# Prompt attention tiles in the order 7, 6, 3, 4, 5, 2, 1, 0, beside a decode whose page loads fill the DMA engines

## The reference, cut to what matters

```python
def diff_attend(q, k, v, q_pos, k_pos, lam):
    s = jnp.einsum('bqhmd,bkhmd->bhmqk', q, k) * (DK_A ** -0.5)
    p = jax.nn.softmax(jnp.where(k_pos[None, :] <= q_pos[:, None], s, -jnp.inf), axis=-1)
    w = p[:, :, 0] - lam * p[:, :, 1]
    return jnp.einsum('bhqk,bkhd->bqhd', w, v)
```

## Time and profile before

| | |
|---|---|
| median of three runs | 973.56 us (973.18 to 977.53) |
| profiled execution: own time / span | 979.25 us / 977.6 us |
| mean granted TensorE clock | 0.986 |
| busy: TensorE, VectorE, ScalarE, GpSimd | 912.6, 493.8, 391.9, 108.9 us |
| moved by DMA | 142.38 MB, 146 GB/s over the span |
| units 8 to 11 (tile 5) on TensorE | 579.07 to 628.79 us |
| units 16 to 19 (tile 3) on TensorE | about 18 us, 670 to 688 us |

### The profile page before, as it was taken

The page is one execution under the profiler, slowest core; times in us unless marked ns, Lnnn a source line. Parts: engine busy times, 40 slices in busy tenths (PEclk is TensorE's granted clock), DMA queues, the critical chain, the costliest instruction groups (busy, mean ns, idle before and its releaser), DMA issues.

```text
span 977.6 us, 18760 instructions
## 1 busy us (share of the span) xinstructions
PE 912.6 (93%) x7095; PEld 738.0 (75%) x7095; DVE 493.8 (51%) x1091; ACT 391.9 (40%) x840; POOL 108.9 (11%) x233
## 2 busy tenths in 40 slices
PE   4989979999999999998789999998979999999996
PEld 3889979999988888887456667775657787587884
DVE  5634744555574355454455655556556444444223
ACT  5533353433335643433544454445554322332211
POOL 1300000000000000002000004343011000000000
PEclk9999999999999999999999999999998999999998
DMA  7362216222332222222976779986984621303221
GB/s 230 96 176 66 66 45 150 67 65 66 97 98 82 86 65 66 86 66 72 357 255 184 240 229 336 334 302 222 319 280 161 234 87 70 95 25 124 86 97 44
DMA packets 115555, 142.38 MB, mean 146 GB/s; under 512 B 9719, under 2 KB 76151, under 8 KB 115466
## 3 DMA queue, kind: packets, MB, share of 16 engines
q1 hardware_dynamic: 109706, 122.31, 39.0%
q0 software_dynamic: 5760, 18.88, 5.4%
HBM read 125.34 MB, written 15.41 MB: 144 GB/s over the span
## 4 chain that ended last, share of the span: by engine, by line
PE 82%; ACT 5%; DMA 4%; DVE 3%; SPq 3%; issue 2%; POOL 0%; POOLq 0%; ACTq 0%; DVEq 0%
PE ps L2003 71%; PE ps L2006 11%; DMA Vr<-in_cache_v 2%; DMA Kr<-in_cache_k 1%; SPq L608 1%; DMA xrow<-in_x_prompt 1%; PE ps L1998 1%; ACT U L955 1%; DMA wst<-in_w_in 0%; ACT whi L930 0%; SPq L598 0%; ACT wh L971 0%; ACT junk L1250 0%; DVE pp L1797 0%; ACT pp L1172 0%
## 5 line engine op out<-in xcount | busy, mean ns | idle before, releaser
L2003 PE MATMUL ps<-hhi,whi 128*128 128x272 f32 (+1 forms) x672 | 227.0, 338 | 2.0 <-DVE hlo L1317 2.0
L2003 PE MATMUL ps<-hhi,wlo 128*128 128x272 f32 (+1 forms) x672 | 217.5, 324 | 0.0
L2003 PE MATMUL ps<-hlo,whi 128*128 128x272 f32 (+1 forms) x672 | 217.0, 323 | 0.0
L2003 PE MATMUL ps<-wh,r 128*128 128x512 f32 x512 | 146.6, 402 | 0.7 <-DVE wout_lo L1863 0.6
L2003 PEld LDWEIGHTS ps<-hhi,whi 128*128 128x128 f32 x672 | 127.2, 189 | 14.8 <-issue 3.7
L2003 PEld LDWEIGHTS ps<-hlo,whi 128*128 128x128 f32 x672 | 127.5, 190 | 9.9 <-issue 1.9
L2003 PEld LDWEIGHTS ps<-hhi,wlo 128*128 128x128 f32 x672 | 127.0, 189 | 9.3
L2003 PEld LDWEIGHTS ps<-wh,r 128*128 128x128 f32 x512 | 95.8, 190 | 23.3 <-issue 1.9
L1333 DVE TENSOR_TENSOR wlo<-wst,whi 128x1024 fp32r<-128x1024 f32 x56 | 68.8, 1229 | 82.0 <-ACT whi L930 82.0
L1762 DVE COPY kTs<-ps 128x512 f32<-128x512 f32 x64 | 44.1, 689 | 71.2 <-PE ps L2006 71.1
L2006 PEld LDWEIGHTS ps<-ident,Kr 128*128 128x128 f32 x512 | 57.1, 143 | 29.2 <-issue 22.0
(11 more groups left out here) (371 smaller groups left out, 1356.5 us busy)
## 6 DMA issues: line engine op xcount, KB each, us to landing
Kr<-in_cache_k SPq DMA_DIRECT2D x128, 256.0 KB, 4.1
wst<-in_w_in SPq DMA_DIRECT2D x56, 512.0 KB, 3.7
Vr<-in_cache_v POOLq DMA_DIRECT2D x72, 256.0 KB, 4.6
Vr<-in_cache_v SPq DMA_DIRECT2D x56, 256.0 KB, 4.4
out_y_prompt<-rows SPq DMA_DIRECT2D x16, 512.0 KB, 2.9
xrow<-in_x_prompt SPq DMA_DIRECT2D x8, 512.0 KB, 4.8
wout<-in_w_out SPq DMA_DIRECT2D x8, 512.0 KB, 5.7
rows<-in_x_prompt SPq DMA_DIRECT2D x8, 512.0 KB, 4.4
```

Of the source, the lines that this page charges most:

```text
L2003: return nc.tensor.matmul(out, lhsT, rhs, start=start, stop=stop, **more)
```

## The change

One line: the list of query tiles. PARTS, DECODED, ATTEND, VALUES_BEFORE and OT are worked out from it.

```diff
 UNITS = CH * H
 PART = 512
-TILES = [7, 6, 5, 4, 3, 2, 1, 0]
+TILES = [7, 6, 3, 4, 5, 2, 1, 0]
 PARTS = [-(-(TILES[u // H] + 1) * P // PART) for u in range(UNITS)]
```

## The result

| | before | after |
|---|---|---|
| median of the runs taken together, us | 974.51 (21 runs, 970.63 to 980.02) | 979.15 (21 runs, 974.01 to 987.31) |
| profiled execution: own time / span, us | 979.25 / 977.6 | 977.63 / 976.0 |

The ratio is 1.0047, 95% interval 1.0029 to 1.0065: 4.6 us slower (2.8 to 6.3). That is clear of zero, and still under the 0.5% that the prediction took for measurable. The forecast was +1.2 us; the median lies inside its range of 970 to 980 us and outside its middle band of 973 to 976.5.

The account below looks back on a forecast made before the run. The prediction took TensorE, with 82% of the chain, to bound the kernel, with DMA close in the key stretch. Its terms, 0 + 0.5 + 5.6 - 2.6 - 2.3 = +1.2 us, gave 974.8 us, range 970.0 to 980.0 us.

Parts of the forecast that it names:

- Point 1: TensorE work moved from units 8 to 13 into units 16 to 21: 5.0 us each way, sum 0.
- Point 2: Key stretch, units 8 to 13: DMA engines full but buffers cover; +0.5 us (0 to +4).
- the +0.5 us for uneven loads: Key stretch: the allowance for uneven loads, with DMA engines expected to be full.
- its 61.5 us for the stretch: Key stretch: time for 22.0 MB at about 358 GB/s, 1.4 us more than TensorE needs.
- The rival of stalled keys: Key stretch: landings pass 10.2 us and TensorE stalls for keys; 978.3 us at the upper end, chance 0.14.
- Point 3: Two-part units 16 to 19 among value steps each wait 1.40 us before second scores; +5.6 us (+1.6 to +6.1).
- Point 4: Units 16 to 21: waits for `head_weights` and value pages go, `wT` waits return in 20 and 21; -2.6 us (-3.0 to -1.0).
- Point 5: Last stretch, after value step 47: SyncE's queue limits the gain to -2.3 us (-3.0 to -0.9).
- the 0.85 us of unit 23's scores: Unit 23's 384-column scores now come behind value step 47, so that step ends 0.85 us sooner.
- The clock falls in units 16 to 19: Units 16 to 19: repeated 1.4 us waits bring two clock falls of some 1.3 us; 977.4 us, chance 0.15.
- The loads run ahead: Last stretch nearly free, second-score waits 0.7 us each; 968.9 us, chance 0.14 in part, 0.07 in full.

Follow-up runs that it names:

- e10: Tile order 7, 6, 2, 1, 5, 4, 3, 0 in place of the kernel before's order, for a lighter key part; 981.84 us in one execution.
- e3: Changed kernel, with VectorE writing the first half of `pp` after only the first part's turning; 976.88 us, ratio 1.0009 to the kernel before.
- e1: Kernel before with tiles 5 and 4 exchanged, inside the key part; 976.75 us, ratio 1.0000.
- e2: Kernel before with tiles 4 and 3 exchanged, so units 16 to 19 have parts of 512 and 128 columns; 979.2 us, ratio 1.0031.
- e11: Changed kernel again with no edit, for a second profile; 983.67 us in one execution.
- e5: Changed kernel with SyncE loading page numbers for value steps 52 to 63 ahead; 978.4 us, ratio 1.0001 to the kernel before.
- e7: Changed kernel with both edits of e3 and e5; 975.06 us, ratio 0.9979 to the kernel before.
- e12: e7 again without further edit, in another session; 974.07 us, ratio 1.0003 to the kernel before.
- e4: Changed kernel with GpSimd issuing value pages up to step 47 instead of 35; 981.2 us, ratio 1.0048 to the kernel before.
- e9: Changed kernel with phase 2's value step or weight turning moved to phase 3 in units 15 to 19; 980.56 us, ratio 1.0046 to the kernel before.
- e6: Kernel before with SyncE loading page numbers ahead, the same edit as e5; 976.59 us, ratio 1.0007.

## Why the prediction came out as it did

**What bounds the kernel** held: TensorE has 84% of the chain (82% before), and each of the differences above is a wait of TensorE or its own work.

**Point 1, right.** The work that left the key part is 5.06 us (4.43 in the stretch and 0.63 ahead of it), forecast 5.0. In the two value stretches busy time grew by 5.18 us (4.64 + 0.54).

**Point 2, key stretch: near in the sum, by luck.** The key step of unit 13 was to come 4.5 us sooner after that of unit 8, and came 4.43 sooner. Two errors offset each other. No part of it was a stall: TensorE lacks 0.42 us there before and after, so the +0.5 us for uneven loads didn't come. And I took the whole 5.0 us of moved work between the borders, though 0.63 us of it lies ahead of the first. The DMA engines took the pace: 384 GB/s at a share of 1.03 over 10 us.

```profile
600.00:610.00 10.00, 10.00 (x130) 7.24 (x132) 5.64 (x14) 4.28 (x9) 3.51 (x7) 1.00 1.03 384
```

The Trainium skill, page "DMA: Bandwidth & Descriptors", section Specifications, gives about 358 GB/s from HBM for a core; the 384 GB/s lie above it, and its 61.5 us for the stretch did not come (60.62). The rival of stalled keys is refuted for this order; e10, one execution, shows it begun at 3.5 us less work.

**Point 3, right.** Four new waits of 1.40 us, 5.6 us in all; with unit 15's, 7.0. The timeline of e3 shows the cause, the waits of e1 and e2 that it belongs to a pair among value steps. One slip: by L1789 the turning that VectorE waits for in unit 15 is that of unit 13's weights, where I wrote 14; the times read are those of the right rows.

**Point 4, nearly right.** The waits for `head_weights` and pages went, as forecast, and the `wT` waits came back in units 20 and 21, but as 0.91 and 0.47 us where I had put them at the old size. That was 0.52 and 0.37 us; the one of unit 16 isn't quite alike, as I had it. Idle time in the value stretch grew by 3.3 us (7.06 less 3.80) against 3.0 forecast, busy time by 4.6 against 4.15.

**Point 5 failed, and it is most of the miss of the first profile.** TensorE's idle time in the last stretch is 5.35 us, and it was 5.36. Of the forecast -2.3 us only 0.3 came (+0.53, less the 0.85 us of unit 23's scores). The mechanism named was right: the stretch is the start of SyncE's queue on step 51, the queue's time from there, and the way from its last issue to the last value step.

| | start | queue | to the last value step |
|---|---|---|---|
| before | 0.8 | 24.3 | 3.7 |
| forecast | 0.2 | 23.5 | 3.7 |
| after | 0.2 | 25.3 | 3.9 |
| after, second profile (e11) | 0.2 | 24.8 | 4.2 |

The step that failed is "I take the lower end". The working gave 23.5 to 24.9 us for the queue, and I chose 23.5 on the argument that its waits for used buffers would go, as TensorE would free them early and run at full speed. In the first profile 2.0 us of such waits are left in the 25.3. But e11 and e3 have only 0.2 us of them, and their queues still take 24.8 and 24.4 us: even without these waits the lower end wasn't reached. What in the queue's own work takes the rest isn't shown.

Two other things differ from the forecast in the first profile. TensorE waited 1.5 us for `on`, the chain of ScalarE's squares, GpSimd's root and VectorE's scale for the prompt's rows, for which the kernel before waits only 0.3 us between 655 and 738 us; and a page wait of 1.76 us was followed by half speed from 723.4 to 726.8, as 1.80 us was before. Neither explains the length: e3 and e11 run at a clock of 1.00 through the whole stretch, wait 0.6 and 0.9 us for `on`, and take 29.0 and 29.1 us, nearly the 29.4 of the first profile. e5, e7 and e12 show the queue's part: with the numbers ahead the same stretch is 2.9, 3.3 and 2.4 us shorter, of which some 1.2 us come back among the value steps ahead of it (46.03 and 45.90 us in e7 and e12, 44.76 in e3).

**The rivals.** "The clock falls in units 16 to 19", given 0.15, is partly true. Of the four profiles of the changed order with full 1.40 us waits three have a stretch of 3.4 us at 0.50 among value steps 27 to 47 (e11 from 677.6, e4 from 682.3, e5 from 674.7) and one, the first, has none. Of the four with the waits of units 16 to 19 cut to 0.55 to 1.10 us (e3, e7, e9, e12) none has one. e10, in another order, has five full waits in a row and no fall. A fall costs 1.6 us where it comes, and it is why e11 is further from the forecast than the first profile. The prediction priced two falls at 2.6 us; there was one. So the falls come with these waits, but that they come from them isn't shown: two profiles of nine speak against it, and the clock was never changed by itself. Nor are such waits the only way to one: e1, which has none of them, has a fall from 692.7 to 696.1, behind a wait of 1.77 us for a page. And the length of a single wait doesn't decide: the prediction set 1.80 us with a fall against 1.53 and 1.40 without, but the 2.03 us of the earlier trace rows have none behind them (clock 1.00 from 694 to 700 us), nor have the 2.40 us of e9. The Trainium skill, page "TensorE: Matmul & The Clock Gate", part 1, has idle time bring the throttle back; here it came back behind repeated gaps of 1.40 us in three profiles of five. "The loads run ahead" fell: it asked for page numbers that cost less, and e5 shows what they cost.

**In sum**: -5.1 us of work out of the key part, +4.6 of busy time among the value steps, +5.6 for the new waits, -2.4 for those that went (less the growth of those for `wT`), and +0.4 in the last stretch (the mean of two profiles) where -1.45 was forecast: +3.2. The measured +4.6 (2.8 to 6.3) leaves 1.4 us, nearly what one fall of the clock costs, and three profiles in four show one. Still open are how often a fall comes in the timed runs, which have no profile, why e9 gains nothing, and what makes the queue longer than the lower end.

## What to carry to other kernels

A phase that hides a wait does so by what stands between its two halves. Before an item is moved from one schedule to another, list for each handshake in it what covered it, and whether the new place has that; here a key step covered 1.40 us, and in units 16 to 19 nothing did. And when waits for data end on a busy queue, removing their cause upstream may return little until the queue's own serial work is shorter (here 0.3 us of 2.3): sum the queue from first issue to last, and where the working leaves a range, don't take the end that supposes all its waits gone.

## What the runs showed of the hardware

- One core took 384 GB/s over 10 us at a DMA share of 1.03 without a late page. In that stretch keys came late only in e10, where 56.7 us of TensorE's work demanded 388 GB/s, with landings of 4.2 to 10.2 us.
- Half speed (a granted clock of 0.50) came behind single waits of 1.76, 1.77, 1.80 and 2.78 us and not behind others of 2.03 and 2.40 us. It came among repeated waits of 1.40 us in three profiles of five. It lasted 3.4 us, and 6.8 us in e6; six fp32 products took 2.72 us in place of 1.60.
- Page numbers for four steps held SyncE's queue 3.1 us after (702.61 to 705.71), beside 0.34 us for a DMA issue.
